# A transformer step's head: modulation columns in pieces of 256, and the first projections taken in four groups of two feature blocks

## The reference, cut to what matters

```python
mod = jnp.dot(jax.nn.silu(cond), w_ada) + b_ada          # 1024 -> 6 x 1024, for two conditions
sh1, sc1, gt1, sh2, sc2, gt2 = jnp.split(mod, 6, axis=-1)
h = _rmsnorm(x, g_pre_mix) * (1 + sc1) + sh1
z = jnp.einsum('bld,de->ble', h, w_in)                    # q, k, v, gates and others
```

## Time and profile before

| | |
|---|---|
| median of 3 runs | 1746.36 us (1746.0 to 1747.34) |
| profiled execution, its own time | 1746.76 us |
| its span in the profile | 1744.9 us |
| PE busy | 1728.8 us (99%) |
| DVE, ACT, POOL busy | 1201.5, 680.1, 266.4 us |
| first matmul of the q product of block 0, of block 1 | 38.43 us, 62.64 us |

### The profile page before, as it was taken

The page is one execution under the profiler, slowest core; times in us unless marked ns, Lnnn a source line. Parts: engine busy times, 40 slices in busy tenths (PEclk is TensorE's granted clock), DMA queues, the critical chain, the costliest instruction groups (busy, mean ns, idle before and its releaser), DMA issues.

```text
span 1744.9 us, 26886 instructions
## 1 busy us (share of the span) xinstructions
PE 1728.8 (99%) x10432; PEld 1626.5 (93%) x10432; DVE 1201.5 (69%) x2547; ACT 680.1 (39%) x1229; POOL 266.4 (15%) x260
## 2 busy tenths in 40 slices
PE   8999999999999999999999999999999999999998
PEld 2998999999999999999988899999999999888887
DVE  4677556566565565364464579888888888798998
ACT  3633221333144143262243454434344444444454
POOL 3010000100000000010000062444433333100000
PEclk9999999999999999999999999999999999999999
DMA  9124334424434455265232331233222222686876
GB/s 346 52 56 141 90 105 128 126 84 145 112 95 159 124 138 185 74 243 170 95 125 94 105 121 66 86 114 110 90 71 72 75 76 76 199 279 221 272 248 246
DMA packets 216275, 236.17 MB, mean 135 GB/s; under 512 B 11568, under 2 KB 160828, under 8 KB 216148
## 3 DMA queue, kind: packets, MB, share of 16 engines
q1 hardware_dynamic: 200916, 179.54, 33.8%
q0 software_dynamic: 10752, 38.00, 6.4%
q10 hardware_dynamic: 4480, 16.91, 2.4%
HBM read 181.49 MB, written 52.92 MB: 134 GB/s over the span
## 4 chain that ended last, share of the span: by engine, by line
PE 90%; DVE 5%; ACT 1%; DMA 1%; issue 1%; SPq 1%; POOL 1%; ACTq 0%; DVEq 0%; POOLq 0%
PE ps L1466 19%; PE ps L1106 13%; PE ps L1107 12%; PE ps L1108 12%; PE ps L1408 6%; PE ps L1483 5%; PE ps L1484 5%; PE ps L1485 5%; PE ps L1273 2%; PE ps L1277 2%; PE ps L1275 2%; PE ps L1289 2%; PE ps L1291 1%; PE ps L1290 1%; DVE mid_g L2647 1%; DVE up_lo L2178 1%
## 5 line engine op out<-in xcount | busy, mean ns | idle before, releaser
L1106 PE MATMUL ps<-H_hi,ring_hi 128*128 128x384 f32 x1200 | 406.5, 339 | 4.7 <-DVE H_lo L2178 4.7
L1107 PE MATMUL ps<-H_lo,ring_hi 128*128 128x384 f32 x1200 | 401.9, 335 | 0.0
L1108 PE MATMUL ps<-H_hi,ring_lo 128*128 128x384 f32 x1200 | 401.8, 335 | 0.0
L1106 PEld LDWEIGHTS ps<-H_hi,ring_hi 128*128 128x128 f32 x1200 | 226.0, 188 | 5.8 <-DVE H_lo L2178 5.5
L1107 PEld LDWEIGHTS ps<-H_lo,ring_hi 128*128 128x128 f32 x1200 | 226.0, 188 | 0.3
L1108 PEld LDWEIGHTS ps<-H_hi,ring_lo 128*128 128x128 f32 x1200 | 225.8, 188 | 0.0
L2355 DVE SCALAR_TENSOR_TENSOR Cst<-Cst,GE,ps 128x257 f32<-128x257 f32 x56 | 26.8, 478 | 163.2 <-PE ps L1277 163.2
L1466 PE MATMUL ps<-T_hi,up_hi 128*128 128x288 f32 x608 | 130.5, 296 | 0.4 <-ACT held_g L2013 0.3
L1466 PE MATMUL ps<-T_hi,up_lo 128*128 128x288 f32 x608 | 130.2, 296 | 0.0
L1466 PE MATMUL ps<-T_lo,up_hi 128*128 128x288 f32 x608 | 130.2, 296 | 0.0
L2178 DVE TENSOR_TENSOR up_lo<-up_raw,up_hi 128x512 fp32r<-128x512 f32 x114 | 89.6, 789 | 57.2 <-ACT up_hi L1971 57.2
(11 more groups left out here) (332 smaller groups left out, 3609.1 us busy)
## 6 DMA issues: line engine op xcount, KB each, us to landing
raw<-in_w_in_dram SPq DMA_DIRECT2D x44, 512.0 KB, 4.1
up_raw<-in_w_up_dram SPq DMA_DIRECT2D x38, 512.0 KB, 5.2
w_raw<-in_w_down_dram SPq DMA_DIRECT2D x66, 256.0 KB, 3.3
raw<-in_w_ada_dram SPq DMA_DIRECT2D x32, 512.0 KB, 5.5
X<-z_f SPq DMA_DIRECT2D x44, 256.0 KB, 3.9
GE<-z_gates SPq DMA_DIRECT2D x72, 128.0 KB, 4.1
w_sub<-in_w_down_dram SPq DMA_DIRECT2D x33, 256.0 KB, 4.0
z_w_diff<-w_raw SPq DMA_DIRECT2D x22, 256.0 KB, 2.5
```

What stands on the lines that cost most here:

```text
L1106: pe.matmul(out, whi, xhi, start=first, stop=False)
L1107: pe.matmul(out, whi, xlo, start=False, stop=False)
L1108: return pe.matmul(out, wlo, xhi, start=False, stop=last)
```

## The change

The 2,048 columns come in eight pieces of 256, piece `r` = 2g holding the shift columns and 2g+1 the scale columns of the feature blocks 2g and 2g+1 (g = 0 to 3). All eight are multiplied on PE, by eight matmuls of 2 x 256 each; the part on DVE and its sum are gone. PE now runs: piece 0, the vector transposes, two norms, piece 1, `ada_cols(0)`. Then for each group g: the q product of two `k`, piece 2g+2, the value product of two `k` for tiles 0 and 1, piece 2g+3, the norms of the next two `k`, `ada_cols(g+1)`, and the value product of tile 2. The last group has no pieces; the transposes of block 1 stand among its six value steps. Block 0 uses banks 0, 1, 2 and 6 at once, the norm turns have two banks in block 0 and three later, and bank 5 holds the rows from piece 2 on. ACT copies the values of block 0 only after it has evacuated all of block 1's norms. The low part of q and both parts of v are made by ACT (`value_hi`) and DVE (`value_lo`). SP loads token block 0 first, then piece 0, q, piece 1, v, v, pieces 2 to 6, token block 1, piece 7, token block 2. The eleven vectors are issued by ACT, before its first activation.

```diff
-    DVE_GROUP, PE_CELLS = 2, 2
-    DVE_CELLS = KD - PE_CELLS
-    ADA_PARTS = (1, 2, 2, 4)
+    FG = 4
+    KG = KD // FG
+    RW = KG * P
+    ADA_PARTS = (1, 2, 1, 1, 1, 1, 1, 1)
...
+    def row_out(r):
+        return ps[0:2, r % 2 if r < 2 else 5, 0:RW] if RW == 512 or r < 2 else ps[0:2, 5, r % 2 * RW:(r % 2 + 1) * RW]
+    def xt_bank(w):
+        return 3 + w % 2 if w < KD else 3 + w % 3
...
+            x_load(0)
+            ada_load(0)
             for n, it in enumerate(raw_items):
+                if n == 1:
+                    ada_load(1)
                 if n == 3:
-                    x_load(1)
+                    for r in range(2, 2 * FG):
+                        if r == 7:
+                            x_load(1)
+                        ada_load(r)
                     x_load(2)
...
+            def ada_rows(r):
+                if r > 2 and (RW == 512 or r % 2 == 0):
+                    pe.wait_ge(row_read, r)
+                for k in range(KD):
+                    if k % (KD // ADA_PARTS[r]) == 0:
+                        pe.wait_ge(ada_part_in(r, k), 16)
+                    mm = pe.matmul(row_out(r), condT[:, :, k], ada_rows_in(r, k), start=(k == 0), stop=(k == KD - 1))
+                mm.then_inc(row_done, 1)
...
             pe.wait_ge(x_scaled, TB)
-            for k in range(4):
-                first_norm(0, k)
+            first_norm(0, 0)
+            first_norm(0, 1)
+            ada_rows(1)
             pe.wait_ge(vec_done, 2)
-            ada_cols(0, 0)
-            ada_cols(1, 8)
-            ada_rows(3, 0, 4)
-            ada_group_sum()
-            ada_cols(DVE_GROUP, 2 * ADA0).then_inc(ada_used, ADA0 // 2)
-            ada_rows(3, 4, KD)
+            ada_cols(0)
+            tiles_of = [[(j, k) for j in range(TB) for k in range(KG * g, KG * (g + 1))] for g in range(FG)]
...
+            for g in range(FG):
+                for k in range(KG * g, KG * (g + 1)):
+                    if k == 0:
+                        pe.wait_ge(lo_ready, 2)
+                    mm = ramp_query(0, k)
+                    if k + 2 < KD and (k + 2) // KG == g:
+                        first_norm(0, k + 2)
+                if g == FG - 1:
+                    mm.then_inc(done0, 1)
+                else:
+                    ada_rows(2 * g + 2)
+                for j, k in tiles_of[g]:
+                    if (j, k) == (0, 0):
+                        pe.wait_ge(lo_ready, 4)
+                    if j == TB - 1 and k == KG * g and g < FG - 1:
+                        ada_rows(2 * g + 3)
+                        for n in range(2):
+                            first_norm(0, KG * (g + 1) + n)
+                        ada_cols(g + 1)
+                    if g == FG - 1:
+                        for n in turns.get((j, k), ()):
+                            if n == 0:
+                                pe.wait_ge(x_scaled, 2 * TB)
+                            first_norm(1, n)
+                    mm = ramp_value(j, (1, 2, 6)[j], k)
+                    if k == KD - 1:
+                        mm.then_inc(done0, 1)
...
             hi_split(1)
+            row_copy(1)
             act.wait_ge(coef1, 1)
-            first_evac(0, range(0, 3))
-            row_copy(3)
-            first_evac(0, range(3, 4))
-            act.wait_ge(coef1, 2)
-            first_evac(0, range(4, KD))
-            x_stats(1)
+            first_evac(0, range(0, 2))
+            value_hi(0)
+            value_hi(1)
+            for g in range(1, FG):
+                if 2 * g == 6:
+                    x_stats(1)
+                row_copy(2 * g + 1)
+                act.wait_ge(coef1, g + 1)
+                first_evac(0, range(KG * g, KG * (g + 1)))
             query_evac(0)
+            first_evac(1)
             value_evac(0)
             value_evac(1)
-            first_evac(1)
             value_evac(2)
...
             scale_x(0)
-            dve.wait_ge(cond_done, 1)
-            ada_group(PE_CELLS, KD)
+            lo_split(1)
             dve.wait_ge(vec_done, 2)
             first_coef(0)
```

More of the change, by code:

```diff
@@ L945, in _ @@
             pool.wait_ge(small_in, 16 * 7)
[L946 to L956, removed]
             pool.wait_ge(ada_used, ADA0)
@@ L1139, in first_norm @@
                 w = b * KD + k
[L1140 to L1170, removed]
+                if w >= 2:
+                    pe.wait_ge(xt_free, w - (1 if b == 0 else 2))
@@ new lines, in ada_cols, with ramp_query @@
+            def ada_cols(group):
+                for r in (2 * group, 2 * group + 1):
+                    pe.wait_ge(row_read, r + 1)
+                    for j in range(KG):
+                        at = 2 * (r % 2 * KD + group * KG + j)
+                        mm = pe.transpose(ps[:, 7, at:at + 2], ada_row[:, r, j * P:(j + 1) * P], ident[0:2, 0:2])
+                mm.then_inc(ada_used, ADA0 // FG)
+            def ramp_query(b, k):
+                pe.wait_ge(h_split_done, b * KD + k + 1)
+                w = slice(k * P, (k + 1) * P)
+                tok = slice(b * BW, (b + 1) * BW)
+                return mm3(ps[:, RQ * b % 3, 0:BW], ring_hi[:, 1, w], ring_lo[:, 1, w], H_hi[:, k, tok], H_lo[:, k, tok],
+                           k == 0, k == KD - 1)
@@ L1172, in _, with ramp_value @@
+            def ramp_value(t, bank, k):
+                tok = slice(t * P, (t + 1) * P)
+                out = ps[:, bank, 0:2 * P + 16]
+                pe.matmul(out, H_hi[:, k, tok], vg0_hi[:, k, :], start=(k == 0), stop=False)
+                pe.matmul(out, H_lo[:, k, tok], vg0_hi[:, k, :], start=False, stop=False)
+                return pe.matmul(out, H_hi[:, k, tok], vg0_lo[:, k, :], start=False, stop=(k == KD - 1))
             pe.wait_ge(cond_done, 1)
             ada_rows(0)
-            ada_rows(1)
@@ new lines, in _ @@
+            tiles_of = [[(j, k) for j in range(TB) for k in range(KG * g, KG * (g + 1))] for g in range(FG)]
+            turn_steps = tiles_of[FG - 1][-KD:]
+            turns = {step: range(KD * n // len(turn_steps), KD * (n + 1) // len(turn_steps)) for n, step in enumerate(turn_steps)}
+            for g in range(FG):
[25 more added lines that the diff above has]
+                        mm.then_inc(done0, 1)
@@ L1196, in _ @@
+            for b in range(1, NB):
                 take0(RQ * b)
                 for k in range(KD):
[L1198 to L1206, removed]
+                    mm = ramp_query(b, k)
@@ L1209, in _ @@
                     q = RQ * b + 1 + j
-                    if b == 0 and j == 0:
-                        pe.wait_ge(lo_ready, 4)
                     take0(q)
-                    tok = slice((b * TB + j) * P, (b * TB + j + 1) * P)
-                    out = ps[:, q % 3, 0:2 * P + 16]
                     for k in range(KD):
@@ L1220, in _ @@
                             first_norm(b + 1, k)
-                        pe.matmul(out, H_hi[:, k, tok], vg0_hi[:, k, :], start=(k == 0), stop=False)
-                        pe.matmul(out, H_lo[:, k, tok], vg0_hi[:, k, :], start=False, stop=False)
-                        mm = pe.matmul(out, H_hi[:, k, tok], vg0_lo[:, k, :], start=False, stop=(k == KD - 1))
+                        mm = ramp_value(b * TB + j, q % 3, k)
                     mm.then_inc(done0, 1)
@@ L1624, in _ @@
             act.dma_start(ident[:, :], consts[:, H_ID:H_ID + P]).then_inc(cond_ident_in, 16)
+            vecA = [b_ada[0], g_pre_mix[0], g_post_mix[0], g_pre_ffn[0], g_post_ffn[0],
+                    g_head[0].rearrange("h v -> (h v)"), pool_scale[0]]
+            at = 0
+            for v in vecA:
+                n = v.shape[0] // P
+                act.dma_start(vecs[at:at + n, 0, :], v.rearrange("(r p) -> r p", p=P)).then_inc(vectors_in, 16)
+                at += n
+            for j, o, v in ((1, 0, conv_w[0, 0]), (1, 44, conv_w[0, 1]), (2, 0, conv_w[0, 2]), (2, 44, conv_b[0])):
+                act.dma_start(vecs[o:o + 44, j, :], v.rearrange("(r p) -> r p", p=P)).then_inc(vectors_in, 16)
             act.wait_ge(rows_turned, 1)
@@ L1682, in value_evac @@
                 q = RQ * (t // TB) + 1 + t % TB
+                bank = (1, 2, 6)[t] if t < TB else q % 3
                 if t == 0:
@@ L1685, in value_evac @@
                 act.wait_ge(done0, q + 1)
-                act.activation(vaug[0][:, t, 0:DV], ps[:, q % 3, 0:DV], ACT.Copy)
+                act.activation(vaug[0][:, t, 0:DV], ps[:, bank, 0:DV], ACT.Copy)
                 act.activation(gate_tok[:, t, :].rearrange("p (g c) -> p g c", c=32)[:, :, 0:4],
-                               ps[:, q % 3, DV:DV + 16].rearrange("p (g c) -> p g c", c=4), ACT.Copy).then_inc(evac0, 1)
+                               ps[:, bank, DV:DV + 16].rearrange("p (g c) -> p g c", c=4), ACT.Copy).then_inc(evac0, 1)
             def gate_evac(b):
@@ L2204, in _, with first_coef @@
             sub_hi(gate_lo, wgate[:, :, :], gate_hi).then_inc(lo_ready, 1)
-            def first_coef(half):
-                dve.wait_ge(ada_used, ADA0 // 2 * (half + 1))
```

(28 more changed lines are left out.)

76 lines of the change are left out of this document (28 added, 48 removed).

## The result

The changed kernel takes 1761.82 us (median of 4 runs, 1760.8 to 1762.55) against 1746.63 (4 runs, 1746.0 to 1747.34): a ratio of 1.0086 with a 95% interval of 1.0069 to 1.0104, slower by 15.2 us. The forecast was 1761.0. The profiled execution of the changed kernel took 1760.8 us of its own, its span is 1759.0 us, 14.1 us more than before. It was the fastest of the four, so the record can show less loss than the median has.

A forecast was written before the change was run, and what follows sets the result against it. PE's list plus its gaps was taken to bound the kernel. Block 1 12.5 us later plus one clock fall of 2.3 gave +14.8 on 1746.8, 1761.6, less part of 0.4 to the median: 1761.0 us; range 1754 to 1769.

The forecast's parts named there:

- The path: After block 1's first product no later wait absorbs a shift, so its delay moves the end by the same amount.
- +12.5 us: Delay of block 1's start, 75.15 instead of 62.64 us, with the clock full all along.
- A piece: Row matmuls of 256 columns on PE: 0.22 us a record, 3.55 us a piece, 28.4 for eight.
- rival (d): Not slower: a piece costs less; at 1.8 us each the +12.5 are gone, below that faster; chance 0.05.
- The growth of PE's list: Row matmuls come from DVE to PE and the group sum goes: about 3.5 us more, all ahead of block 1.
- The start: Before group 0: `wgate` holds DVE until 14.15 us, x scaled at 17.5, first q matmul at 25.2 instead of 38.43.
- The groups: From one q product to the next: 13.85 us a period, with 1.8 us of PE idle in the chain.
- The bank wait: Before block 1's q product, PE waits for ACT's copy of tile 0, behind eight evacuations of 5.6 us: 1.95 us lost.
- The clock: One fall to the lower level in the idles from 21.8 to 25.2 us, before the first q: 2.3 us.
- rival (b): The clock falls in the groups too: two more falls give 1766 us, one in every group 1768.5; chance 0.14.

The follow-up runs named there:

- Experiment 3: Changed kernel with half the work of pieces 2 to 7 left out (four of eight feature blocks multiplied): 1751.88 us, ratio 1.0027.
- experiment 1: Changed kernel with DVE's wait for `wgate` and split of the gate weights moved behind the scaling of the first token block: 1760.56 us, ratio 1.0078.
- experiment 7: Changed kernel with POOL again making the low part of q and both parts of v, instead of ACT and DVE: 1764.56 us, one run.
- experiment 2: Changed kernel with ACT copying tile 0 of block 0 after four of block 1's eight evacuations, not after all: 1761.41 us, ratio 1.0083.
- Experiment 9: Changed kernel with gate split behind the first scaling, earlier copy of tile 0, and filler matmuls in PE's idles, also before the norms: 1756.26 us, ratio 1.0055.
- experiment 6: Changed kernel with small identity matmuls filling PE's idles before piece 0 and before each group, none before the norms: 1762.25 us, ratio 1.0084.
- experiment 4: Changed kernel in two groups of four feature blocks, pieces of 512 columns, a row copy per piece, token block 1 before the last piece: 1761.11 us.
- experiment 5: Kernel before with only POOL's weight splits moved to ACT and DVE: 1746.97 us, ratio 0.9997.
- experiment 8: Kernel before with POOL's splits moved and placed in gaps, q and v loads reordered, short PE waits filled: 1742.88 us against 1746.91, ratio 0.9978.

## Why the prediction was right

**The path.** Nothing after block 1's start took up the shift; in the profiles the whole difference lies before 76.84 us. Without the clock the forecast had +12.5 us, and the record has 14.2 - 1.7 = 12.5. That this agrees to 0.1 us is in part luck: the periods ran 0.8 us longer than their sum and the bank wait 1.0 shorter.

**A piece** was put at 3.55 us between bounds of 1.9 and 7.1. A piece at full clock shows as 3.62 with its tail, and its successor starts 3.54 after it. Experiment 3 shows that it is paid one for one. That settles rival (d): the line through the rows of 512 and 128 columns holds at 256. The growth of PE's list stands in the forecast once at 3.5 us and once, in the ledger, at 3.3; by its own price of a piece it is 28.4 - 23.4 - 1.95 = 3.05. The +12.5 don't rest on it.

**The start.** x scaled at 17.5, first q at 25.2: measured 17.5 and 25.31. The cause, `wgate` at 14.15 (14.26 after), is shown by experiment 1.

**The groups.** 13.85 us a period: measured 13.95, 15.73 and 14.35. The second has the fall of the clock in it (piece 4 took 5.29 us). The forecast had 1.8 us of idle in each; the first two have 1.5. The two tiles of values take 1.7 us, not 1.5. The third has 0.3 of extra wait (1.80): the cast takes 0.66 us there at 68.03, while POOL issues two DMAs (67.19 to 68.51). In experiment 7 they end 0.2 us into the cast, and it takes 0.38; that POOL's issues are the cause is suggested by this, not tested.

**The bank wait** was put at 1.95 us and measured 0.97, the term that was most off: ACT's eight evacuations took 5.02 us, not 5.6 as in the earlier trace rows (those 5.6 are the pace of PE's transposes before, which start every 0.70 us from 57.00 on; four evacuations with nothing to wait for take 2.38 us in experiment 2), and the copy behind them 0.45 instead of 0.56; PE's last values ended 0.1 later in the group than worked out. The wait itself, and its place, are shown by experiment 2, and by 9 against 6.

**The clock.** The forecast had one fall, near 23 us, at 2.3 us. The record of the changed kernel has two. One began near 10.1 us, in the wait for piece 0, whose 4.89 us instead of 3.62 were hidden behind the wait for x. The other began at 40.9 us and cost 1.7 us. So one fall was paid, but in another place and at less: the count is the forecast's, the place, in the groups, is rival (b)'s. The reason given for the place was misread from the record before. There the fall did not follow two idles; it came between them, at 43.1 us, after the idle of 2.15 us and 0.9 us of matmuls. In windows (length; PE, PEld, DVE, ACT, POOL busy; clock; DMA), the kernel before:

```profile
42.19:43.10 0.91, 0.91 (x6) 0.84 (x6) 0.91 (x1) 0.00 (x0) 0.91 (x1) 1.00 1.01 394
43.10:45.22 2.12, 0.29 (x3) 0.00 (x1) 2.09 (x4) 0.00 (x0) 2.12 (x3) 0.50 1.13 323
```

In the changed kernel it came at 40.9 us, 1.6 us behind the end of an idle of 1.50. In experiments 1, 2 and 7 it did come in the idle before group 0 or right after it. The Trainium skill's warning of idle gaps (TensorE: Matmul & The Clock Gate, "Why this matters for your kernels") names idle gaps as the cause of drops. The trace and experiment 6 agree with it in kind; the gaps behind which the clock fell here, 1.50 us in the changed kernel and 2.15 before, are shorter than those it warns of, and the measurement decides. Which idle it takes differs by run, and the profile and the medians differ too: 12.5 of waits and list plus 1.7 are 14.2, which is the profile's 76.84 - 62.64; the medians differ by 15.2. What the medians have beyond the profile is not known, since the other executions have no record.

**What wins nothing and what loses.** First features came 13 us earlier and the casts became short. Against that stand 5.4 - 1.95 us of matmuls that DVE had done beside PE, a later first matmul, and four chains of columns, coefficients, ACT and DVE, each with 1.5 to 2.6 us in which PE has nothing. Experiment 9 takes away the wait for `wgate`, the bank wait and the falls, not these four chains: 1756.3, so 5.6 of the 15.2 us were those. What is left is the list, the later first matmul and the chains, in which PE now runs fillers. Of these, experiment 3 shows the price of the list; the price of a chain is read from the record, and experiment 4, with two chains fewer, agrees with it but changes other things as well.

## What to carry to other kernels

When the busiest engine is nearly full through a stage, sum its list before and after first: work that moves onto it is paid one for one, and earlier first results give nothing back unless its idles shrink by more. Cutting a stage into more groups repeats the chain between groups once for each, so hand-overs of 2 us belong into the sum with their count. And a fix that removes contention is worth only what the order around it lets through: taking the splits off POOL gave 0 us with the moved operations in one place, and 4 with them in another, the loads reordered and the short waits filled; which of these three made the difference was not tested.

## What the runs showed of the hardware that was not expected

The clock fell in a stretch with little idle time of PE. In experiments 5 and 8 it went to its lower level (1.2 GHz) near 34.5 us, behind 3 us in which PE was busy for 2.62 (the windows of experiment 8), with 16 matmuls of one column and 4 transposes of two columns. In the kernel before the same operations stand at the same place, and its record shows no fall there. One thing differs in PE's rows: in experiments 5 and 8 PE waits 0.39 and 0.38 us for `group_part` just before the small matmuls, and in the kernel before it hardly waits:

```profile
31.10:34.10 3.00, 2.90 (x23) 2.30 (x23) 0.52 (x4) 0.83 (x1) 0.00 (x0) 1.00 1.21 291
```

Whether that short wait, the small matmuls or chance made the fall was not tested.

Filling one idle can move the fall to the next. In experiment 6, with fillers of 2.3 us ahead of it, piece 0 ran at full clock and ended 1.4 us earlier than in the changed kernel, and in the wait behind it, now 3.06 us, the clock went down and cost 2.9 us. With three more fillers there, x scaled earlier and that wait down to 0.33 us, the clock stayed full up to block 1 (experiment 9). One record each does not make this a rule: in experiments 1, 2 and 7 piece 0 ran at full clock without fillers (3.61 us), and in 2 and 7 idles of 2.54 and 2.94 us at the same place passed without a fall.
